# Another order at the joints of five feed-forward layers, and one weight sum of three of them moved from VectorE to an accumulating transfer

## The reference

```
def swiglu(x, w_gu, w_down):                      # D = 1024, D_FF = 2816
    gate, up = jnp.split(x @ w_gu, 2, axis=-1)
    return (jax.nn.silu(gate) * up) @ w_down

first_block:   attention + pooling, memory attention, h = h + swiglu(rmsnorm(h))        # layer 0
second_block, for l in (0, 1):
    h = h + 0.5 * rmsnorm(swiglu(rmsnorm(h, g0), ...), g1)                               # layers 1 and 3
    h = h + rmsnorm(mix(rmsnorm(h, g2)), g3)      # a gated convolution, then differential attention
    h = h + 0.5 * rmsnorm(swiglu(rmsnorm(h, g4), ...), g5)                               # layers 2 and 4
```

## Time and profile before

| | |
|---|---|
| median of 3 runs | 1267.11 us (1266.94 to 1269.29) |
| the profiled execution | 1267.36 us |
| its span, first to last instruction | 1265.5 us |
| PE busy | 1250.5 us, 5897 matmuls |
| DVE busy | 1042.0 us |
| ACT busy | 804.2 us |
| POOL busy | 194.5 us |
| read from memory | 275.24 MB, 218 GB/s over the span |

### The profile page before, as it was taken

One profiled execution on the slowest core, in us unless ns is written; L12 is line 12 of the kernel. 1 busy time (PEld: TensorE's weight loads), 2 busy tenths in 40 slices (PEclk: granted clock), 3 DMA queues, 4 the chain that ended last, 5 costly groups with the idle time before them and its releaser, 6 DMA issues.

```text
span 1265.5 us, 15538 instructions
## 1 busy us (share of the span) xinstructions
PE 1250.5 (99%) x5897; PEld 1029.7 (81%) x5897; DVE 1042.0 (82%) x1035; ACT 804.2 (64%) x986; POOL 194.5 (15%) x224
## 2 busy tenths in 40 slices
PE   9999999999999999999999999999999999999998
PEld 7888878888888878888788888888888877788886
DVE  6766689999789996757799997999977568999984
ACT  6674576666576664645766664766656467766662
POOL 6142130110001100202201101111001003301100
PEclk9999999999999999999999999999999999999999
DMA  9537498997649955568979978389745535999931
GB/s 335 174 101 227 131 315 255 260 270 262 199 144 252 268 171 196 177 238 204 330 248 245 273 249 262 118 239 274 218 166 179 182 123 172 314 288 260 266 135 45
DMA packets 143002, 277.32 MB, mean 219 GB/s; under 512 B 8992, under 2 KB 39896, under 8 KB 142928
## 3 DMA queue, kind: packets, MB, share of 16 engines
q1 hardware_dynamic: 120192, 229.67, 51.5%
q0 software_dynamic: 22288, 45.54, 19.4%
q10 hardware_dynamic: 448, 1.12, 0.2%
HBM read 275.24 MB, written 1.05 MB: 218 GB/s over the span
## 4 chain that ended last, share of the span: by engine, by line
PE 83%; DVE 10%; issue 3%; ACT 3%; DMA 1%; POOL 0%; DVEq 0%; POOLq 0%; SPq 0%; ACTq 0%
PE B L2102 14%; PE B L2104 14%; PE B L2103 14%; PE B L2560 7%; PE B L2558 7%; PE B L2559 7%; DVE w_lo L1359 5%; PE T L2102 3%; PE T L2104 3%; PE T L2103 3%; PE T L2582 1%; DVE VD L1378 1%; ACT w_hi L768 1%; ACT w_hi L1082 1%; DMA VD<-in_ffn_w_gu 1%
## 5 line engine op out<-in xcount | busy, mean ns | idle before, releaser
L1359 DVE TENSOR_TENSOR w_lo<-w_raw,w_hi 128x2048 fp32r<-128x2048 f32 x129 | 296.5, 2300 | 87.2 <-ACT w_hi L768 86.9
L768 ACT ACTIVATE w_hi<-w_raw 128x2048 fp32r<-128x2048 f32 x129 | 247.2, 1919 | 103.2 <-PE B L2560 60.7
L2102 PE MATMUL B<-w_hi,xt_lo 128*128 128x512 f32 x652 | 260.2, 399 | 4.3 <-DVE w_lo L1359 2.2
L2104 PE MATMUL B<-w_hi,xt_hi 128*128 128x512 f32 x652 | 254.5, 390 | 0.0
L2103 PE MATMUL B<-w_lo,xt_hi 128*128 128x512 f32 x652 | 254.1, 390 | 0.0
L2558 PE MATMUL B<-w_hi,act_lo 128*128 128x512 f32 x440 | 172.5, 392 | 0.6 <-DVE w_lo L1359 0.6
L2560 PE MATMUL B<-w_hi,act_hi 128*128 128x512 f32 x440 | 171.4, 390 | 0.0
L2559 PE MATMUL B<-w_lo,act_hi 128*128 128x512 f32 x440 | 171.3, 389 | 0.0
L2102 PEld LDWEIGHTS B<-w_hi,xt_lo 128*128 128x128 f32 x652 | 122.5, 188 | 34.6 <-issue 4.4
L2104 PEld LDWEIGHTS B<-w_hi,xt_hi 128*128 128x128 f32 x652 | 122.4, 188 | 26.2
L2103 PEld LDWEIGHTS B<-w_lo,xt_hi 128*128 128x128 f32 x652 | 122.6, 188 | 23.2
(11 more groups left out here) (330 smaller groups left out, 2113.1 us busy)
## 6 DMA issues: line engine op xcount, KB each, us to landing
w_raw<-in_ffn_w_down SPq DMA_DIRECT2D x88, 512.0 KB, 5.7
Z<-in_ffn_w_gu SPq DMA_DIRECT2D x64, 512.0 KB, 7.8
w_raw<-in_ffn_w_gu SPq DMA_DIRECT2D x48, 512.0 KB, 5.1
nat<-in_ffn_w_gu SPq DMA_DIRECT2D x32, 512.0 KB, 7.7
QT<-in_ffn_w_gu SPq DMA_DIRECT2D x32, 512.0 KB, 7.0
Z<-in_ffn_w_gu POOLq DMA_DIRECT2D x32, 512.0 KB, 8.6
w_raw<-in_conv_w_in SPq DMA_DIRECT2D x24, 512.0 KB, 4.9
w_raw<-in_w_down SPq DMA_DIRECT2D x22, 512.0 KB, 6.4
```

The lines of the kernel that those rows point to most:

```text
L768: act.activation(whi[home(u)][:, :], raw[slot][:, :], ACT.Copy).then_inc(w_hi, 1)
L1359: dve.tensor_tensor(wlo[home(u)][:, :], src, whi[home(u)][:, :].bitcast(F32), ALU.subtract).then_inc(w_lo, 1)
L2102: pe.matmul(bank[:, :], lo[:, k, x], whi[s][:, c], start=first, stop=False, skip_group_check=more)
L2104: return pe.matmul(bank[:, :], hi[:, k, x], whi[s][:, c], start=False, stop=last, skip_group_check=more)
```

## The change

For f = 1, 3 and 4 T4 of the first pair is made by an accumulating transfer of POOL; DVE's sum is left out, and SP's load of B21 no longer waits for it. The other edits change orders:

- the start of each layer but f = 1: DVE splits N1b before x_sums; f = 0 sums the first token tile of the input earlier, in place of both at once; in every layer ACT does the gates before it copies the input sums; f = 0 and 4 have a tiny Silu ahead of the gates; f = 4 sums its squares after the copy for N1b
- into f = 2: the split of unit U_COUT + 5 goes between the two halves of the squares (ACT) and of the products with the post gain (DVE)
- into f = 4: DVE splits U_O + 4 before heads_lo(3), and PE does the products of the heads for the second token tile in another order, with one product fewer between the last pair of heads and the turns

```diff
+FIRST_T4 = (1, 3, 4)
+def added_t4(f):
+    return ((0,) if f in FIRST_T4 else ()) + ADDED_T4
 def sums_of(f):
-    return (((0, "T1"), (0, "T2")) if f % 2 else ()) + ((0, "T4"),) + SUMS
+    return (((0, "T1"), (0, "T2")) if f % 2 else ()) + (() if f in FIRST_T4 else ((0, "T4"),)) + SUMS
 def t4_added(f, p):
-    return 32 * (len(ADDED_T4) * f + ADDED_T4.index(p) + 1)
+    return 32 * (sum(len(added_t4(g)) for g in range(f)) + added_t4(f).index(p) + 1)
...
# SP, next_block
-                        if name == "B21" and p == 0:
+                        if name == "B21" and p == 0 and f not in FIRST_T4:
                             sp.wait_ge(t_ok, sums_ready(f, 0, "T4"))
# POOL, add_blocks
+                if p0 and 0 in added_t4(f):
+                    add_block("T4", f, 0, w_gu)
                 for p in range(p0, SQUARES):
                     add_block("T3", f, p, w_gu)
-                    if p in ADDED_T4:
+                    if p in added_t4(f):
                         add_block("T4", f, p, w_gu)
# ACT, sum_squares
-                tok_squares(stat, lambda t, half: pairs[half][t][:, :], 0,
-                            [sum_done(reader, u_last, 0, half) for half in range(2)])
+                waits = [sum_done(reader, u_last, 0, half) for half in range(2)]
+                tok_squares(stat, lambda t, half: pairs[half][t][:, :], 0, waits, (0,))
+                split_at(*between)
+                tok_squares(stat, lambda t, half: pairs[half][t][:, :], 0, waits, (1,))
# ACT, ffn
-                    if f == 4:
-                        h_squares(stat, reader, 0)
-                    h_squares(stat, reader, 1)
+                    if f != 4:
+                        h_squares(stat, reader, 1)
...
-                    elif src == "T4" and p in ADDED_T4:
+                    elif src == "T4" and p in added_t4(f):
                         act.wait_ge(t4_in, t4_added(f, p))
...
                 weights("N1b")
+                if f == 4:
+                    for t in range(TOKS):
+                        h_squares(stat, reader, t)
                 block("P1", 0)
+                if f in (0, 4):
+                    act.activation(table[:, f // 4:f // 4 + 1], gains[:, G_ONE:G_ONE + 1], ACT.Silu)
+                act.wait_ge(rstd, 2 * ST[stat] + 2)
+                gate_of(0, u0 + OP["N0b", 0], PAIR[0] if f else F0)
                 act.wait_ge(sx_ok, f + 1)
                 act.wait_ge(w_used, u0 + OP["N0b", 0] + 1)
                 act.activation(yhi[:, :, :], xsum, ACT.Copy).then_inc(sx_hi, 1)
-                act.wait_ge(rstd, 2 * ST[stat] + 2)
-                gate_of(0, u0 + OP["N0b", 0], PAIR[0] if f else F0)
# ACT and DVE, into f = 2
-            split_at(*range(U_COUT + 2, U_COUT + 6))
-            sum_squares("y1", "ffn2", U_COUT + 3, (), n2(0, 4), early=8)
+            split_at(*range(U_COUT + 2, U_COUT + 5))
+            sum_squares("y1", "ffn2", U_COUT + 3, (), n2(0, 4), early=8, between=(U_COUT + 5,))
...
-            ffn(2, "h5", "ffn2", n2(0, 4), lambda t: post_update(1, "y1", "ffn2", t))
+            ffn(2, "h5", "ffn2", n2(0, 4), lambda t: post_update(1, "y1", "ffn2", t, between=() if t else (U_COUT + 5,)))
# DVE, post_update
                     ins = dve.tensor_tensor(tmp[:, half, :], pairs[half][t][:, :], gpost[:, c], ALU.mult)
+                    if half == 0:
+                        split_at(*between)
# DVE, into f = 0, and ffn
+            x_total("ffn0", 0, 1)
             split_at(21)
...
-                if f == 0:
-                    total = x_total(reader)
-                else:
+                if f:
...
-                    total = x_total(reader, 1, 2)
+                total = x_total(reader, 1, 2)
...
-                x_sums(total)
-                weights("N1b")
+                if f == 1:
+                    x_sums(total)
+                    weights("N1b")
+                else:
+                    weights("N1b")
+                    x_sums(total)
...
-                weight_sum("T4", f, 0)
+                if f not in FIRST_T4:
+                    weight_sum("T4", f, 0)
...
-                    if p not in ADDED_T4:
+                    if p not in added_t4(f):
                         weight_sum("T4", f, p)
# DVE, into f = 4
+            split_at(U_O + 4)
             heads_lo(3)
-            split_at(U_O + 4, U_O + 5)
+            split_at(U_O + 5)
# PE, into f = 4
             heads_pair(3)
-            for k in (4, 5):
-                out_heads(0, k, 1)
+            for half in range(2):
+                for k in (4, 5):
+                    out_heads(half, k, 1)
             pe.wait_ge(ao_lo, 4)
...
             for k in (6, 7):
                 out_heads(0, k, 1)
-            for k in (4, 5):
-                out_heads(1, k, 1)
+            out_heads(1, 6, 1)
             turn("ffn4", 0, 0, h, h_waits("ffn4"))
             turn("ffn4", 0, 1, h, h_waits("ffn4"))
-            out_heads(1, 6, 1)
+            out_heads(1, 7, 1)
             turn("ffn4", 0, 2, h, h_waits("ffn4"))
             turn("ffn4", 0, 3, h, h_waits("ffn4"))
-            out_heads(1, 7, 1)
             ffn(4, "ffn4", h_waits("ffn4"), turned=True)
```

More of the change, by code:

```diff
@@ L221, in build @@
         lam4 = sb("lam4", [P, 4])
+        table = sb("silu_of_one", [P, 2])
         SS = sb("row_squares", [P, len(ST), TOKS, 2])
@@ L782, in turned_hi, with tok_squares @@
                                    scale=gains[:, g:g + 1]).then_inc(xt_hi, 1)
-            def tok_squares(stat, src, t, waits):
-                for half in range(2):
+            def tok_squares(stat, src, t, waits, halves=(0, 1)):
+                for half in halves:
                     if waits:
@@ L795, in h_squares, with sum_squares @@
                 tok_squares(stat, lambda t, half: h[:, t, half * HALF:half * HALF + HALF], t, waits)
-            def sum_squares(stat, reader, u_last, late_split=None, gain=0, pairs=PAIR, early=4):
-                tok_squares(stat, lambda t, half: pairs[half][t][:, :], 0,
-                            [sum_done(reader, u_last, 0, half) for half in range(2)])
+            def sum_squares(stat, reader, u_last, late_split=None, gain=0, pairs=PAIR, early=4, between=()):
+                waits = [sum_done(reader, u_last, 0, half) for half in range(2)]
+                tok_squares(stat, lambda t, half: pairs[half][t][:, :], 0, waits, (0,))
+                split_at(*between)
+                tok_squares(stat, lambda t, half: pairs[half][t][:, :], 0, waits, (1,))
                 if late_split is not None:
@@ L1403, in turned, with x_total @@
                 split_at(u0 + 2)
+            def x_total(name, t0=0, t1=TOKS):
+                dve.wait_ge(xt_lo, XT[name] + t1 * KD)
+                x = slice(t0 * P, t1 * P)
+                steps[0] += 1
+                dve.tensor_tensor(xsum[:, :, x], xhi[:, :, x].bitcast(F32), xlo[:, :, x].bitcast(F32), ALU.add)\
+                    .then_inc(dve_step, 1)
+                return steps[0]
             def evac(e, u_last, dst, pair, stat):
@@ L1437, in h_update, with post_update @@
                     dve.tensor_tensor(part, part, pairs[half][t][:, :], ALU.add).then_inc(h_up, 1)
-            def post_update(b, stat, reader, t, pairs=PAIR):
+            def post_update(b, stat, reader, t, pairs=PAIR, between=()):
                 if t == 0:
@@ L1729, in kv_round_lo @@
                 ins.then_inc(kv_lo, 1)
-            def x_total(name, t0=0, t1=TOKS):
-                dve.wait_ge(xt_lo, XT[name] + t1 * KD)
-                x = slice(t0 * P, t1 * P)
-                steps[0] += 1
-                dve.tensor_tensor(xsum[:, :, x], xhi[:, :, x].bitcast(F32), xlo[:, :, x].bitcast(F32), ALU.add)\
-                    .then_inc(dve_step, 1)
-                return steps[0]
             def x_sums(total):
```

## The result

| | before | changed |
|---|---|---|
| median | 1267.68 us (1266.94 to 1269.29, 4 runs) | 1281.15 us (1280.77 to 1282.57, 4 runs) |
| profiled execution, its span | 1267.36 us, 1265.5 us | 1281.44 us, 1279.6 us |

The ratio is 1.0104, 95% interval 1.0091 to 1.0117. The changed kernel is slower by 13.5 us. The direction is that of the forecast; 1281.15 is 0.15 above the end of its range; by the ratio, from the 1267.11 us that the forecast started at, it is 1280.3, inside. The loss is 1.8 times the 7.4 to 7.6 us forecast.

A forecast was written before the change was run, and what follows sets the result against it. PE is busy nearly throughout, with DVE's order the hidden bound before D1. Transfer +10.5, orders -2.3, -0.5 and -0.3 give +7.4 us on 1267.36 or the median 1267.11: 1274.7 us, range 1269 to 1281 (likeliest case 1271 to 1281).

The forecast's parts named there:

- those ahead of P7: PE's waits of 0.25 us before P7 in three layers would go, 0.4 us each with restart, inside D1's loss.
- The price of the transfer: First pair, P6's split to ACT's copy: 11.53 us in f = 1, 10.29 in f = 3 and 4; 10.5 us lost in all.
- SP's earlier B21: Second pair's load, no longer waiting for DVE's sum: queued behind B22 on the same queue, so it adds nothing.
- After D1 both queues stand to each other as before, so I give nothing back.: Behind D1 of the first pair, ACT's and DVE's queues: D1's losses of 4.3, 3.1 and 3.1 us stay, none recovered.
- the very upper bound: Whole kernel: transfer loss at most 15 us, less 1.5 us of least gains from the orders, so +13.5 us.
- The rival of the clock: PE's clock falls to 1.2 GHz for D1 or half of it, 16 or 8 us in three layers: 1283 to 1291; chance 0.08.
- The rival of the hidden transfer: First pair's second half lands 6.5 us after issue, copy hardly put off: 1263.0 us; chance 0.11.
- The orders: Gains: 2.3 us at N1b of f = 0, 2, 3, 4; 0.5 into f = 2; 0.3 into f = 4.
- the 0.3 taken there: Into f = 4, PE's wait of 0.65 us for h: reordered splits and head products gain 0.3, from -0.3 to 0.9.

The follow-up runs named there:

- experiment 5: Changed kernel with SP's load of B21 for the second pair held until the first pair's T4 transfer has landed (f = 1, 3, 4): 1285.28 us, ratio 1.0147.
- Experiment 6: Changed kernel with SP's loads of B22, B21 and B12 for the second pair all held until the T4 transfer has landed: 1283.75 us, ratio 1.0135.
- experiment 2: Kernel before with only T4 of the first pair by transfer in f = 1, 3 and 4, in the old orders: 1283.09 us, ratio 1.0117.
- experiment 3: Changed kernel with DVE's C22 and C12 ahead of P4's split and T1 behind act_lo, first pair of f = 1, 3, 4: 1280.19 us, ratio 1.0087.
- Experiment 7: Changed kernel with the first pair's T4 transfer in f = 1, 3, 4 a plain copy without the addition: 1265.93 us, ratio 0.9994.
- experiment 1: Changed kernel with T4 of the first pair back on DVE in every layer, so the new orders alone: 1264.78 us, ratio 0.9971; repeated, 1265.27 us, 0.998.
- experiment 4: Changed kernel with 11 unused identity matmuls on PE between P4 and D1 of the first pair in f = 1, 3, 4: 1282.6 us, ratio 1.011.

## Why the prediction was right, and where its size was off

**What bounds the stretch.** The prediction read off that DVE's order holds D1 up with 0.25 us to spare, and that lateness of P4's split goes on to PE. This held: the waits came where it put them, and those ahead of P7 went. Their sizes were divided otherwise: 0.40 to 3.17 ahead of P4, for 0.4 to 1.7 forecast, and 1.15 to 2.69 ahead of D1, for about 3.

**The price of the transfer: the term that was mis-sized.** "What it takes from there is shown by the same transfer for p = 1 and 2." From issue to copy it took these:

| f | assumed | measured | D1's loss forecast | D1's loss measured |
|---|---|---|---|---|
| 1 | 11.15 | 12.69 | 4.3 | 4.72 + 1.03 = 5.75 |
| 3 | 9.91 | 11.73 | 3.1 | 9.66 - 4.84 = 4.82 |
| 4 | 9.91 | 10.12 | 3.1 | 12.38 - 9.01 = 3.37 |

The copy was later by 1.54 + 1.82 + 0.21 = 3.6 us and D1 by 13.9 - 10.5 = 3.4. So the chain from the transfer to D1 was worked out rightly, and the transfer's own time was not. Which load it shares the queues with was named rightly too: SP's earlier B21 adds nothing, as experiment 5 shows, and B22 does, as 6 against 5 shows. The mistake is that p = 1 and 2 were taken for the same surroundings.

B22 is loaded beside the transfer for p = 1 and 2 too, but not as close behind it. SP issues it when P3's split is done. In the first pair DVE goes from P6's split straight or nearly straight to P3's, in the kernel before too (P3's split starts at 372.28 there, right behind P6's); for p = 1 and 2 of the layers it pauses 0.3 to 0.9 us for ACT between them. SP's timelines, of the kernel before for the p = 2 of the earlier trace rows, and of the changed kernel for f = 1, p = 0:

```profile
434.65 0.97 SPq L425 DMA_DIRECT2D nat<-in_ffn_w_gu  x2
```
```profile
373.55 1.17 SPq L432 DMA_DIRECT2D nat<-in_ffn_w_gu  x2
```

| adding transfer | B22's load behind POOL's issue | second half lands | issue to copy |
|---|---|---|---|
| before, f = 1, p = 2 | 2.26 | 10.4 | 11.15 |
| before, f = 4, p = 1 | 2.40 | 9.2 | 9.91 |
| changed, f = 1 | 1.98 | 11.9 | 12.69 |
| changed, f = 3 | 2.01 | 10.9 | 11.73 |
| changed, f = 4 | 2.14 | 9.4 | 10.12 |
| experiment 2, f = 4 | 1.97 | 11.3 | 12.02 |
| experiment 3, f = 4, p = 1 | 1.93 | 11.3 | 12.05 |

In the traces of all runs together the second half of such a T4 transfer took 10.7 to 11.9 us in the 14 cases in which B22 was issued 1.93 to 2.04 us behind the transfer, and at most 10.8 wherever it was 2.14 or more. The last two rows have slow transfers where the changed kernel had fast ones (10.12 and 9.97), so it is neither the layer nor the pair. It is also how a delay feeds itself: in experiment 3 DVE lags behind ACT, pauses no longer between the splits of P6 and P3 of the second pair, and the next transfer is slow as well. This is read from the traces; no run moved B22's load by itself, and why some tenths of a us matter so much is not shown.

**"After D1 both queues stand to each other as before, so I give nothing back."** This step was wrong, and in the direction opposite to a gain: the lag grew further, by 1.57, 0.29 and 1.72 us behind D1, and only 0.6 of it was given back in f = 1. Part of it goes with the fallen clock, about 1.6 us in each of f = 1 and 4. In all T4 cost 16.9 us by the trace, 10.5 forecast: 3.4 more from the transfer's time, 3.0 more from what came behind D1.

**How much of it was luck.** The mechanism was right, and the direction with it. That the time still fell about at the edge of the range is in part luck: +13.5 us is the very upper bound that the prediction added up, and the clock's share in the measured loss, some 1.6 us in each of f = 1 and 4 behind D1, stands in no term of that bound. The prediction itself named a fall of the clock as a sign that it would be wrong.

**The rival of the clock.** It was half right. The clock did fall, in each of the three layers, behind waits of 2.2 to 2.7 us. But about 8 matmuls ran at the low level each time, 1.6 us, where the rival had half or all of D1's 24: 4.8 us in three layers in place of 8 to 16, and in f = 3 they ran inside P4, where PE then waited for act_lo anyway. The Trainium skill, TensorE: Matmul & The Clock Gate, section "HAM oscillation — how this bites in real kernels", warns of this; the trace agrees that it happens here. The forecast and this rival were not alternatives; waits like those that the one computed bring the other about.

**The rival of the hidden transfer.** It needed 7 us from P6's split to the copy. Experiment 6 bounds it from below: alone on the queues the adding transfer needs 8.6 to 8.8 us from its issue, so no holding back of SP's loads would have hidden it. Experiment 7 shows that a plain one can nearly be: its copy started 6.35 us behind the issue in f = 1, having waited 0.38.

**The orders.** Forecast 2.3 + 0.5 + 0.3 = 3.1; the lag fell by 1.03, 0.68, 0.60 and 0.60 us at the N1b of f = 0, 2, 3 and 4, and by 0.48 at the turn into f = 2; within f = 2 0.9 was lost again, at three starts behind DVE's splits. The same 0.9 goes in f = 2 of experiment 1, so it does not come from the transfer; what makes those splits late nothing here shows. Into f = 4 the wait stayed, so the 0.3 taken there are nought. Experiment 1 measured 2.5 to 3.7 in all, so the sum came out right while one of its terms was nought.

**What stays open.** How the 3.0 us behind D1 divide between the clock and the splits that DVE still brings late: experiment 3 removed the wait at D1 in all three layers and the fall in f = 1 and 4 (in f = 3 it stayed, inside P4), experiment 4 kept the fall out of D1 but had it in P4 of f = 1 and 3, and neither came out faster by what it removed. For experiment 3 the late transfers of the second pair account for 5.3 us of that.

## What to carry to other kernels

Taking work off an engine is worth what the bounding engine waited for it, here about 1.3 us by the traces (0.6 to 1.8 by the times) for 6.8 us of DVE's time, and the thing put in its place is paid in full wherever the receiving engine has no slack. Before a sum is handed to an adding transfer, take its time from the same transfer with the same loads beside it and as close behind it, and count it as nearly twice its bytes on the queues. When an engine's queue is full, look at its idle time over the whole round, not only at who waits first: reordering moves the first wait and leaves the sum.

## What the runs showed of the hardware

- An accumulating transfer of 1 MB from memory into on-chip memory, with nothing beside it, needed 8.6 to 8.8 us from issue to use at 182 to 187 GB/s, with the DMA engines' share at 1.04 to 1.12; with one plain load of 1 MB behind it, 12.0 to 12.6 in two of three layers and 9.98 in the third (experiment 5), where that load came 2.14 us behind in place of 1.97. The same bytes as a plain copy landed in 3.9 to 5.5 us each half, with the load beside it at up to 336 GB/s. A plain load issued 1.93 to 2.04 us behind the start of an adding transfer went with 10.7 to 11.9 us for its second half, one issued 2.14 us or more behind it with at most 10.8.
- The page of the kernel before had the rate in it. Queue, packets, MB, and share of 16 engines' span:

```profile
q1 hardware_dynamic: 120192, 229.67, 51.5%
q0 software_dynamic: 22288, 45.54, 19.4%
```

  Over 1265.5 us SP's queue moved 229.67 MB in 651.7 us of its packets' time, 352 GB/s, and POOL's, where most transfers add, 45.54 MB in 245.5 us, 185 GB/s.
- PE's clock fell for about 8 matmuls after two waits close together that summed to 3.1 us (0.40 and 2.69, f = 4) and to 5.9 us (3.17 and 2.68, f = 1), and after one of 2.16 us (f = 3). In experiment 7 it fell after one of 2.20 us and not after one of 0.51. The length of one wait does not decide it: in f = 1 P4 ran at full clock behind 3.17 us, and in experiment 4 at half behind 2.62.
